# A hybrid SSM and DeltaNet block: another order of weight splits, decay loads and buffer waits, and a norm weight multiplied in at the eviction

## What is computed

```python
h = rms_norm(x, g_mix_pre)
z, xbc, dt, qkv, gate, b, a, m_gate = split(h @ w_in)          # 8192+ columns
y_ssm = mamba2_branch(z, xbc, dt, ...)                          # chunks of tokens, a state carried on
y_gdn = gdn_branch(qkv, gate, b, a, ...)                        # chunks, a triangular solve in each
mixed = sigmoid(m_gate)[0] * (y_ssm @ w_br_ssm) + sigmoid(m_gate)[1] * (y_gdn @ w_br_gdn)
x = x + rms_norm(mixed @ w_out, g_mix_post)                     # the out-projection and its norm
h = rms_norm(x, g_ffn_pre)
x = x + rms_norm((gelu(conv(h @ w_gate)) * (h @ w_up)) @ w_down, g_ffn_post)
x = x + rms_norm(sigmoid(x @ w_ple_gate) * (p @ w_ple_proj), g_ple_post)
```

## Time and profile before

| what | value |
|---|---|
| median of three runs | 2745.88 us (2745.42 to 2748.67) |
| the profiled execution | 2739.36 us, of which the span is 2737.2 us |
| TensorE busy | 2586.7 us, 95% |
| VectorE busy | 1448.4 us, 53% |
| GpSimd busy | 1052.1 us, 38% |
| ScalarE busy | 532.7 us, 19% |
| HBM traffic | 111 GB/s over the span |
| granted clock of TensorE, mean | 0.975 |

### The profile page before, as it was taken

How to read it: one execution, slowest core, us unless ns; L and a number is a source line. 1 busy time by engine, 2 the same in 40 slices (tenths; PEclk the granted TensorE clock), 3 DMA queues, 4 the chain that set the end, 5 groups by cost and what they waited for, 6 DMA issues and landing times. The chain is left out here.

```text
span 2737.2 us, 29514 instructions
## 1 busy us (share of the span) xinstructions
PE 2586.7 (95%) x12016; PEld 2117.9 (77%) x12016; DVE 1448.4 (53%) x1183; ACT 532.7 (19%) x540; POOL 1052.1 (38%) x549
## 2 busy tenths in 40 slices
PE   6999999799989999989998799999999999999995
PEld 5888888577768888868876588888888888888774
DVE  4779776123665656741426744444444444444755
ACT  4100111345412323230013200000000000000432
POOL 2334332344535555523454433333333333333361
PEclk8999999899999999999998999999999999999997
DMA  5322222577866675653232211111111111111231
GB/s 197 105 95 85 100 92 86 188 235 247 276 176 185 182 212 150 172 169 138 92 138 93 93 46 47 47 46 46 55 52 46 46 46 46 46 46 61 93 108 62
DMA packets 276942, 304.06 MB, mean 111 GB/s; under 512 B 43821, under 2 KB 241786, under 8 KB 272762
## 3 DMA queue, kind: packets, MB, share of 16 engines
q1 hardware_dynamic: 246122, 248.88, 29.3%
q10 hardware_dynamic: 30736, 54.01, 5.4%
HBM read 216.35 MB, written 86.51 MB: 111 GB/s over the span
## 5 line engine op out<-in xcount | busy, mean ns | idle before, releaser
L436 PE MATMUL ps<-act_hi,w_hi 128*128 128x512 f32 x2288 | 912.3, 399 | 31.4 <-POOL w_lo L423 18.8
L440 PE MATMUL ps<-act_hi,w_lo 128*128 128x512 f32 x2288 | 906.2, 396 | 0.0
L439 PE MATMUL ps<-act_lo,w_hi 128*128 128x512 f32 x2288 | 901.7, 394 | 0.0
L421 POOL TENSOR_SCALAR w_hi<-w_raw 128x1024 fp32r<-128x1024 f32 x219 | 247.3, 1129 | 1412.5 <-PE ps L436 605.3
L423 POOL TENSOR_TENSOR w_lo<-w_raw,w_hi 128x1024 fp32r<-128x1024 f32 x219 | 575.1, 2626 | 18.3
L436 PEld LDWEIGHTS ps<-act_hi,w_hi 128*128 128x128 f32 x2288 | 433.8, 190 | 133.0 <-issue 24.2
L439 PEld LDWEIGHTS ps<-act_lo,w_hi 128*128 128x128 f32 x2288 | 433.8, 190 | 100.2 <-issue 3.6
L440 PEld LDWEIGHTS ps<-act_hi,w_lo 128*128 128x128 f32 x2288 | 433.8, 190 | 90.6
L2013 DVE TENSOR_TENSOR tile<-ps,tile 128x1024 f32<-128x1024 f32 x112 | 135.6, 1221 | 108.0 <-PE ps L1574 106.5
L2451 DVE SCALAR_TENSOR_TENSOR ring_a<-xin,par,ring_a 128x1024 f32<-128x1024 f32 x108 | 183.2, 1696 | 11.8 <-DVE ring_a L2445 0.3
L1574 PE MATMUL ps<-f_hi,w_lo 128*128 128x512 f32 x480 | 189.1, 394 | 0.0
(11 more groups left out here) (287 smaller groups left out, 2886.1 us busy)
## 6 DMA issues: line engine op xcount, KB each, us to landing
w_raw<-in_w_in_dram SPq DMA_DIRECT2D x34, 1024.0 KB, 5.4
spill<-ring_b ACTq DMA_DIRECT2D x67, 512.0 KB, 2.7
w_raw<-in_w_ffn_gate_dram SPq DMA_DIRECT2D x17, 1024.0 KB, 5.4
w_raw<-in_w_ffn_up_dram SPq DMA_DIRECT2D x17, 1024.0 KB, 5.4
w_raw<-in_w_ffn_down_dram SPq DMA_DIRECT2D x16, 1024.0 KB, 4.8
qkv_a<-spill SPq DMA_DIRECT2D x8, 1536.0 KB, 6.9
dec_a<-cum_rows SPq DMA_DIRECT2D x16, 512.0 KB, 12.5
gdn_in<-hrow SPq DMA_DIRECT2D x8, 1024.0 KB, 14.6
```

Source lines behind the costliest of these rows:

```text
L421: nc.gpsimd.tensor_scalar(hi, raw, 1.0, 0.0, ALU.mult, ALU.add).then_inc(split_done, 1)
L436: first = nc.tensor.matmul(o, wh, mov[0][:, k, c], start=(k == 0), stop=False)
L439: nc.tensor.matmul(o, wh, mov[1][:, k, c], start=False, stop=False)
L440: last = nc.tensor.matmul(o, wl, mov[0][:, k, c], start=False, stop=(k == KD - 1))
```

## The change

In the Z stretch GpSimd splits units 0 and 1 before its loop, unit 2 and unit 3 ahead of the decays of chunk 0; SyncE issues the decay loads of each chunk ahead of the waits for spills and `a_qk` and of the rows; ScalarE evicts unit 1 after the first norms instead of after the squares of chunk 1. In the mixer GpSimd splits the third gate unit and unit 0 of the mixer ahead of the decays of chunk 0, and each later split one place earlier; TensorE multiplies the whole of unit 0 before `invert_r(0)`, and chunks 4 and 5 have 8 steps instead of 12; the evictions and the weight blocks move to match; SyncE's wait for the spills follows the first loads. At the out-projection ScalarE multiplies by g_mix_post while it evicts, in two instructions of 512 tokens, so that VectorE multiplies a pair by the factor in one tensor_tensor, and adds the pair before; `first_gu` waits for each buffer just before it writes it.

```diff
--- before.py
+++ after.py
@@ -624,11 +624,11 @@
 
         ready_to_mix(sp)
         sp.wait_ge(d_kept, 16 * 8)
-        for k in range(2):
-            sp.wait_ge(spilled[k], uses_spilled(J_MG, k))
         sp.wait_ge(zeroed, 2)
         load_inv(0)
         load_dec(0)
+        for k in range(2):
+            sp.wait_ge(spilled[k], uses_spilled(J_MG, k))
         load_xbc(0)
         load_qk(0)
         load_bv(0)
@@ -639,7 +639,7 @@
         block_load(3)
         load_inv(1)
 
-        blocks_at = {0: 4, 2: 5, 3: 6, 4: 7, 6: 8, 7: 9}
+        blocks_at = {0: 4, 1: 5, 3: 6, 4: 7, 6: 8, 7: 9}
         for c in range(NCH):
             load_g(c)
             if c < NCH - 1:
@@ -700,16 +700,17 @@
         for t in (nt, dd):
             g.memset(t[:, :, :], 0.0).then_inc(zeroed, 1)
         split_unit(pool, U_MG, 1)
+        split_unit(pool, U_MG, 2)
         ready_to_mix(pool)
         for t in (s_ssm, s_gdn):
             g.memset(t[:, :, :], 0.0).then_inc(zeroed, 1)
-        split_unit(pool, U_MG, 2)
+        mg_split(0)
         decays(0)
-        mg_split(0)
+        mg_split(1)
         decayed_x(0)
-        mg_split(1)
-        split_first = {0: 2, 1: 4, 2: 5, 3: 7, 4: 8, 5: 10, 6: 11, 7: 12}
-        split_last = {0: 3, 2: 6, 4: 9}
+        mg_split(2)
+        split_first = {0: 3, 1: 5, 2: 6, 3: 8, 4: 9, 5: 10, 6: 11, 7: 12}
+        split_last = {0: 4, 2: 7}
         for c in range(NCH):
             states(c)
             skip_x(c)
@@ -782,7 +783,7 @@
             return m[:, g * HPG:(g + 1) * HPG, :].rearrange("p h d -> p (h d)")
 
         def main(c, more):
-            steps = (2, 2, 2, 2, 2, 1, 1) if c < 6 else (2, 1, 1, 1, 1, 1, 1)
+            steps = (2, 2, 2, 2, 2, 1, 1) if c < 4 else (2, 1, 1, 1, 1, 1, 1)
             after(pe, in_qk, c * 16 + 16)
             after(pe, bs_copied, c + 1)
             after(pe, s_gdn_new, c * 2)
@@ -858,6 +859,7 @@
         pe.wait_ge(zeroed, 4)
         for b in range(1, NBUF):
             pe.wait_ge(tile_free[b], used_ahead(O_MIX, b))
+        gemm(KD)
         invert_r(0)
         gemm(2)
         x_rows_of(0)
@@ -909,15 +911,15 @@
             for batch in range(2):
                 after(act, vn_done, c * 2 + (batch + 1))
                 a(flat(rhs[:, heads_of(batch), :]), bank(PA + batch), ACT.Copy).then_inc(vn_copied, 1)
-            if c in (1, 3, 5):
-                mg_evict({1: 2, 3: 5, 5: 8}[c])
+            if c in (1, 3):
+                mg_evict({1: 3, 3: 6}[c])
             after(act, o_sum, c * 2 + 2)
             after(act, y_out, c)
             a(sqs[:, :, :], qs[:, :, :], ACT.Square).then_inc(osq_done, 1)
             if more:
                 copy_r(c + 1)
-            if c in (0, 2, 4):
-                mg_evict({0: 1, 2: 4, 4: 7}[c])
+            if c in (0, 2):
+                mg_evict({0: 2, 2: 5}[c])
             after(act, y_mid, c * 2 + 2)
             after(act, o_ssq, c + 1)
             a(sqs[:, :, :], yssm[:, :, :], ACT.Square).then_inc(ysq_done, 1)
@@ -938,8 +940,8 @@
             act.dma_start(y_c[:, 0:KD, tokens(c)], yssm[:, :, :]).then_inc(ys_kept, 16)
             after(act, yg_out, c + 1)
             act.dma_start(y_c[:, KD:2 * KD, tokens(c)], gt[:, :, :]).then_inc(yg_kept, 16)
-            if c in (1, 3, 5, 6, 7):
-                mg_evict({1: 3, 3: 6, 5: 9, 6: 10, 7: 11}[c])
+            if c in (1, 3, 4, 5, 6, 7):
+                mg_evict({1: 4, 3: 7, 4: 8, 5: 9, 6: 10, 7: 11}[c])
 
         for m in range(MG_PLAIN):
             j = J_MG + m
@@ -951,10 +953,11 @@
             act.dma_start(spill[j], ring_b[:, j % 2, :]).then_inc(spilled[j % 2], 16)
         d_store(act, 1)
         ready_to_mix(act)
+        mg_evict(0)
         copy_r(0)
         copy_bs(0)
         exp_dec(0)
-        mg_evict(0)
+        mg_evict(1)
         inverse_kept(act)
         for c in range(NCH):
             main(c, c < NCH - 1)
@@ -1173,6 +1176,8 @@
         squares(0)
         for c in range(NCH):
             norms(c)
+            if c == 0:
+                evict(1)
             decays(c, 0)
             if c:
                 evict(2 * c)
@@ -1181,7 +1186,8 @@
                 squares(c + 1)
             else:
                 d_store(act, 0)
-            evict(2 * c + 1)
+            if c:
+                evict(2 * c + 1)
         a_ended(act)
         for b in range(2):
             act.sem_inc(tile_free[b], 8)
@@ -1233,11 +1239,14 @@
 
     def pool_a(pool):
         g = nc.gpsimd
-        split_unit(pool, U_A, 0)
+        for m in range(2):
+            split_unit(pool, U_A, m)
         for m in range(2 * NCH):
             c, nth = m // 2, m % 2
             i = c % 2
-            if m < 2 * NCH - 1:
+            if m < 2:
+                split_unit(pool, U_A, m + 2)
+            elif 3 < m + 1 < 2 * NCH:
                 split_unit(pool, U_A, m + 1)
             if m == 0:
                 pool.wait_ge(tm_kept, len(TM_COLS))
@@ -1258,18 +1267,18 @@
 
         def loads(c):
             i, tok = c % 2, slice(c * P, c * P + P)
-            for k in range(2):
-                sp.wait_ge(spilled[k], uses_spilled(J_Z, k))
             sp.wait_ge(tm_kept, len(TM_COLS))
-            after(sp, a_qk, 2 * c)
-            after(sp, a_vt, c)
-            sp.dma_start(qkv_a[:, :, :], spill_c[:, J_Q:J_Q + QKV_T, tok]).then_inc(a_in, 16)
             sp.wait_ge(cum_kept, 16)
             after(sp, kept_d[i], 16 * (c // 2))
             after(sp, kept_n[i], 64 * (c // 2))
             for loaded, row, at in ((a_dn, ROW_U, 8), (a_dq, ROW_A, 0)):
                 sp.dma_start(dec_a[:, i, at:at + 8, :], cum_rows[row:row + GDN_HEADS, tok].unsqueeze(0).broadcast_to([P, GDN_HEADS, P])
                              ).then_inc(loaded[i], 16)
+            for k in range(2):
+                sp.wait_ge(spilled[k], uses_spilled(J_Z, k))
+            after(sp, a_qk, 2 * c)
+            after(sp, a_vt, c)
+            sp.dma_start(qkv_a[:, :, :], spill_c[:, J_Q:J_Q + QKV_T, tok]).then_inc(a_in, 16)
 
         def stores(c):
             i = c % 2
@@ -1398,6 +1407,7 @@
     ADDED = [s for s in SQUARES if s[2]]
     RS_COUNT = {("n1", 0): 1, ("n2", 0): 2, ("n1", 1): 3, ("n2", 1): 4, ("n3", 0): 5, ("n3", 1): 6, ("n4", 0): 7, ("n4", 1): 8}
 
+    X1_STEP = {"A0": 3, "A1": 5, "A2": 7, "A3": 8}
     STEP = {"S0": 1, "S1": 2, "S2": 3, "S3": 4, "A0": 5, "S4": 6, "S5": 7, "A1": 8, "S6": 9, "S7": 10, "A2": 11, "A3": 12}
 
     def acc_of(name, h):
@@ -1603,10 +1613,12 @@
 
         def first_gu():
 
-            bufs = [wait_buffer(pe, O_F0, n) for n in range(4)]
+            bufs = [uses(O_F0, n)[0] for n in range(4)]
             for n in range(4):
+                wait_buffer(pe, O_F0, n)
                 pe_half(pe, U_F0 + n, ps[:, 2 * bufs[n], :], 0, mov, (lambda k: L_FFN + k // 2 + 1) if n == 0 else None)
                 if n == 0:
+                    wait_buffer(pe, O_F0, 3)
                     pe_sum(pe, ps[:, 2 * bufs[3] + 1, :], "n1", 1).then_inc(late_sum, 1)
             pe_sum(pe, ps[:, 2 * bufs[2] + 1, :], "n2", 1).then_inc(late_sum, 1)
             for n in range(4):
@@ -1758,11 +1770,13 @@
             if h + m == 0:
                 act.wait_ge(lo_done, L_MIX + KD)
             square("n1", h, m, by_two(buf(b)))
-            a(pair_of(tile3, h, m), by_two(buf(b)), ACT.Copy).then_inc(tile_free[b], 1)
+            for i in range(2):
+                out = a(tile3[:, 2 * m + i, in_half(h)], ps[:, 2 * b + i, :], ACT.Copy, scale=pcol("g_mix_post", 2 * m + i))
+            out.then_inc(tile_free[b], 1)
 
         def x1_squares(h):
             for m in range(4):
-                act.wait_ge(x1_step, 12 * h + STEP[f"A{m}"])
+                act.wait_ge(x1_step, 8 * h + X1_STEP[f"A{m}"])
                 square("n2", h, m, pair_of(tile3, h, m))
             act.dma_start(x1_cm[:, :, in_half(h)].rearrange("k q t -> q k t"), tile3[:, :, in_half(h)]).then_inc(x1_kept, 16)
 
@@ -1928,14 +1942,21 @@
                 mixed_low(j - 1)
         mixed_low(KD - 1)
 
-        def x1_add(h, m, base):
-            dve.wait_ge(res_in[0], 16)
-            v.tensor_tensor(pair_of(tile3, h, m), pair_of(tile3, h, m), pair_of(res3, h, m), ALU.add).then_inc(x1_step, 1)
-
         def out_norm(h):
+
+            def add(m):
+                dve.wait_ge(x1_step, 8 * h + X1_STEP[f"A{m}"] - (2 if m < 3 else 1))
+                v.tensor_tensor(pair_of(tile3, h, m), pair_of(tile3, h, m), pair_of(res3, h, m), ALU.add).then_inc(x1_step, 1)
             b, c = uses(O_WO_PAIR[h][3], 0)
             dve.wait_ge(tile_free[b], c + 1)
-            scale_add(tile3, "g_mix_post", "n1", h, x1_step, x1_add)
+            dve.wait_ge(norm_rs, RS_COUNT["n1", h])
+            dve.wait_ge(res_in[0], 16)
+            rs = rs_of("n1", h).unsqueeze(1).broadcast_to([P, 2, HALF])
+            for m in range(4):
+                v.tensor_tensor(pair_of(tile3, h, m), pair_of(tile3, h, m), rs, ALU.mult).then_inc(x1_step, 1)
+                if m:
+                    add(m - 1)
+            add(3)
 
```

## The result

The changed kernel takes 2727.6 us (median of four, 2726.3 to 2735.7) where the kernel before took 2747.3 us (four runs) beside it: ratio 0.9946, 95% interval 0.9929 to 0.9963, so 14.8 us less, where 29 were forecast. Of the executions reported here two are slow ones and not counted (2778.7 and 2944.7 us of e2, at a granted clock of 0.93 and 0.84). The profiled execution is the slowest of the four, 2735.7 us (span 2734.0).

A forecast was written before the change was run, and what follows sets the result against it. TensorE, busy for 95% of the span, was taken as the bound, so only its idle spots could be won. Gains of 18 (Z stretch), 4 (mixer) and 7 us (out-projection) made 29, giving 2717 us, range 2702 to 2736.

The forecast's parts named there:

- Part 1: Z stretch: splits, decay loads and an eviction reordered; 18 us gained (8 to 25).
- block 2: Z stretch: weight block issued at 521.5, split done by 532, so the 5.61 us gap at unit 4 goes.
- the landing of the rows: Z stretch, chunk 0: rows land at 493 behind the decay pair, leaving TensorE idle 8.4 us before the sums.
- the other end of the sum: Z stretch, chunk 0: rows land at 498 if the decay pair is slow; 8 us gained at unit 4, not 13.
- Part 2: Mixer: unit 0 multiplied whole early, chunks 4 and 5 shortened; 4 us gained (0 to 8).
- The wait for the store: Mixer start: TensorE idle from 796.3 to 802.3 before unit 1, until ScalarE evicts unit 0; one 6 us gap.
- The split beside the substitution: Mixer start: one more GpSimd split falls beside VectorE's substitution, costing 0.5 us.
- The short chunks: Mixer chunks 4 and 5 with 8 steps: 4.6 us gained each, 1.5 off for chunk 6 behind a short one.
- The third rival: Mixer: short chunks 4 to 6 meet decays 3 us late; part 2 is -4, 21 us gained in all, chance 0.15.
- The first rival: Z stretch stays bound by the DMA queue, rows at 498; part 1 gives 6, 17 us in all, chance 0.2.
- Part 3: Out-projection norm: 6 us from the order of buffer waits, 1 from the weight; 7 us gained (4 to 11).
- The second rival: Z stretch: rows come late in every chunk behind the decay loads; 6 us slower, 2752, chance 0.07.

The follow-up runs named there:

- e2: Only the mixer's changes, put into the kernel before: ratio 1.0002, 0.5 us slower.
- f1: The changed kernel with SyncE issuing the rows of chunk 0 ahead of its decay loads: ratio 0.9910, 24.7 us faster than the kernel before.
- second trace: Another profiled execution of the changed kernel, unaltered, from the follow-up experiments: 2723.9 us.
- g2: Changed kernel, chunk 0 rows first, mixer eviction and copies before the store, plus chunks 4 to 6 gate eviction before the exponential: 0.9931 of the kernel before.
- all three edits: Changed kernel with chunk 0 rows first, unit 0 eviction and copies before the substitution's store, GpSimd's mixer decays halved: ratio 0.9881 to the kernel before.
- version with eviction first: Changed kernel with ScalarE's eviction of mixer unit 0 and rinv copies ahead of the substitution's store: ratio 0.9914, 23.6 us faster than the kernel before.
- first trace: The profiled execution of the changed kernel, unaltered, slowest of its four: 2735.7 us.

## Why the prediction was wrong

The measured time, 2727.6 us, lies inside the stated range (2702 to 2736), but the gain is half of the forecast. The steps that failed are terms of the sum, in parts 2 and 3 above all.

**Part 1, 18 us: nearly right in its sum, by two errors that cancel; 12.9 in the time.** The splits ahead, the eviction and block 2 did as said (1.4 us left at unit 4). The failed term is the landing of the rows, said to be 493, with the two decay tiles down 10.7 us after their issue as in the pair of the earlier trace rows. They are down after 16.0 us, the rows 5.8 us later, at 495.9 in an execution that was 1.8 us early: the other end of the sum (498). TensorE's wait is 13.2 us, not 8.4. So chunk 1 has 8.5 us, 6.7 without what lies ahead of the stretch, where 13 were forecast for unit 4, and 8 by that other end. The later chunks gave 9.9 where 5 were forecast: TensorE's idle time from the Gram products of chunk 1 to those of chunk 7 went from 9.4 to 4.2 us, and the rest no row shows. The rule by which the sum would go to 498, of the Trainium skill (DMA: Bandwidth & Descriptors, "Queues, rings and completion order"), is borne out by the row and by f1. The rows behind the broadcast were named, priced and accepted in the sum, but not as an order to undo: it is worth 10 us. That the two errors nearly cancel is luck.

**Part 2, 4 us: wrong, 0.** The wait for the store was named and sized at 6 (8.8 and 7.8 measured). The split beside the substitution was a term of 0.5 us and measured 3.0: the split's two GpSimd instructions (1.05 and 2.4 us) were counted in part, though VectorE's instructions beside them last as long as they do. The Trainium skill (SBUF — State Buffer, "SBUF: two separate sides") says just this of two-input instructions of VectorE beside a GpSimd instruction that reads SBUF; it was used for part 3 and not here. The short chunks were forecast at 9.2 less 1.5, from chunk 6 alone. Chunk 6 stood behind a long one, and the tile comes 32 to 36 us after a chunk's start, long or short, followed by some 10 us of GpSimd and ScalarE and VectorE's product. Measured are 5.9 us from chunk 0 to 7 in the second trace and 1.0 in the first. Over all traces these seven chunks take 317.0 to 318.9 us in the old order and 310.3 to 319.9 in the new one with all its work (326.6 in g2). The third rival ("the mixer loses", each short chunk meets its decays late) had this mechanism; its chance was 0.15. Its time, 2725, is near the measured one by luck, since it stands for 21 us gained and 14.5 to 14.8 were. The first rival, congestion stays, was nearest in gain (17 us) and right on the rows at 498, but not on part 1, which it put at 6.

**Part 3, 7 us: mechanism right, size wrong.** For the buffer waits 6 us stood in the sum; 2.2 to 5.2 came in the traces. The meeting with the split was priced right (2.2, measured 2.7 us: two instructions of L1972 take 4.16 us, of before 1.41). What was not counted is the wait that is left (3.7, or 1.5 and 2.9 us) and the slow clock behind it in some executions, although had priced it. The weight was put at 2 us and gives 0.6. In the time both together are 1.6 us, not told from nothing.

**The sum.** 29 = 18 + 4 + 7; measured alone 12.9, -0.5 and 1.6. Part 1 in the time is 2.5 us less than in its own stretch (15.4 in its trace), which the interval of the time, 3.3 us either way, covers.

**The checks.** Right: no long waits for units 2, 3 and 4; the split of unit 2 (474.9 to 478.4 us, said 476); one gap in front of unit 1 of the mixer, released by ScalarE. VectorE's waits for stores in chunks 3 to 6 (16.7, 14.4, 3.6 and 3.3 us before) are gone. Wrong: rows at 493, "about 8 us" before the sums, chunk 5 at 41 to 43 us (45.6 and 47.7; over 45 was a sign of being wrong), no wait at the out-projection. The second rival, rows late in every chunk, didn't come: the one wait over 2 us of the later chunks is the 4.1 before chunk 7's Gram products, for VectorE beside the substitution.

## What to carry to other kernels

When loads are reordered, ask of each what it delays and who is first in need; a slow repeated-row load goes behind whatever TensorE waits for, which a single chunk's exception may give. A chunk made shorter on the bound engine exposes the longest chain from load to use: compare that chain with the chunk's new length before counting the steps saved. Two places in one engine's list, each found in one row of the changed kernel's profile, were worth 24 us by the ratios and 16 by the two profiled executions, more than all the rest of the change (14.5).

## What was not expected of the hardware

One execution (all three edits, 2723.8 us where its four siblings took 2702.4 to 2713.2) ran its matmuls of the feed-forward stage 1.9% slower at a granted clock of 1.00: 859 instead of 875 started in 200 us, with no wait. The same stretch of that trace and of the version with eviction first:

```profile
1700.00:1900.00 200.00, 200.00 (x859) 162.01 (x858) 90.07 (x60) 12.73 (x12) 64.76 (x36) 1.00 0.15 47
```

```profile
1700.00:1900.00 200.00, 200.00 (x875) 164.12 (x874) 90.16 (x60) 12.74 (x12) 64.98 (x36) 1.00 0.15 47
```

What causes it no run shows. And the clock behind an idle spot of the same length (3.67 us at the out-projection, in the first trace and in f1) was 0.58 once and 1.00 once, which moves a step by 2 us or more; stages that no edit touches differ by as much and more from one execution to the next. A profile alone doesn't settle a gain of that size.
